# Two products for three, ScalarE's first parts ahead of POOL, and a weight ring of three and three slots

## What is computed

```python
h = rms_norm(x, pre_norm_gain); proj = h @ w_in            # q k v z_a b c u z_c, 512 columns each
mixed = concat([attn, conv_out]) @ w_out; x = x + rms_norm(mixed, post_norm_gain)
x = x + sigmoid(x @ w_ple_gate) * rms_norm(p @ w_ple_proj, ple_norm_gain)
n = rmsnorm(h, norm_mix); parts = n @ w_in2                # c_q c_kv k_pe gq gk gv ga gg gate_a gate_b
mix = sigmoid(gate_a) * (y_a @ w_o_mla) + sigmoid(gate_b) * (y_b @ w_o_gla); h = h + mix @ w_out2
q = rmsnorm(h, norm_ffn) @ w_q; s = q . sub_keys; top 16 of 128 for both halves, then top 16 pairs
out = sum over experts of gate * gelu(h . u) * v           # dense here: 16384 experts in 128 tiles
```

## Time and profile before

| | before |
|---|---|
| median of 3 runs | 2176.15 us |
| span of the profiled execution | 2175.93 us |
| TensorE busy | 2115.4 us, 97% |
| VectorE, ScalarE, POOL busy | 1304.1, 922.6, 1033.5 us |
| DMA | 359 MB, 165 GB/s in the mean |

### The profile page before, as it was taken

The page is one execution under the profiler, slowest core; times in us unless marked ns, Lnnn a source line. Parts: engine busy times, 40 slices in busy tenths (PEclk is TensorE's granted clock), DMA queues, the critical chain, the costliest instruction groups (busy, mean ns, idle before and its releaser), DMA issues.

```text
span 2175.9 us, 27394 instructions
## 1 busy us (share of the span) xinstructions
PE 2115.4 (97%) x10296; PEld 1661.6 (76%) x10296; DVE 1304.1 (60%) x2244; ACT 922.6 (42%) x1528; POOL 1033.5 (47%) x892
## 2 busy tenths in 40 slices
PE   8999999999999999999999998999999899999999
PEld 6877767557887776887878877777778788888887
DVE  6456257352235774215898957888881666666664
ACT  4223343572234234111334447777773434343432
POOL 6655546212324122877859887999996100000000
PEclk9999999999999999999999999999999999999999
DMA  5222312201111111233216664777788988888884
GB/s 201 100 78 78 116 61 90 90 30 49 59 40 59 59 55 43 97 122 110 78 59 199 205 206 141 272 289 246 272 291 294 333 300 286 289 284 300 288 287 149
DMA packets 98291, 359.32 MB, mean 165 GB/s; under 512 B 8480, under 2 KB 41504, under 8 KB 73328
## 3 DMA queue, kind: packets, MB, share of 16 engines
q1 hardware_dynamic: 98160, 357.56, 47.3%
HBM read 286.09 MB, written 71.30 MB: 164 GB/s over the span
## 4 chain that ended last, share of the span: by engine, by line
PE 67%; POOL 13%; DVE 11%; issue 6%; ACT 2%; DMA 1%; POOLq 0%; SPq 0%; ACTq 0%; DVEq 0%
PE ps L1438 11%; PE ps L1439 11%; PE ps L802 10%; PE ps L803 9%; PE ps L804 9%; POOL area L2643 6%; POOL wring_parts L2621 6%; PE ps L791 2%; PE ps L1249 2%; DVE area L2413 2%; PE ps L1386 1%; PE ps L1387 1%; DVE area L2410 1%; PE ps L884 1%; PE ps L1225 1%
## 5 line engine op out<-in xcount | busy, mean ns | idle before, releaser
L2577 POOL CAST wring_parts<-wring 128x512 fp32r<-128x512 f32 x236 | 170.5, 764 | 546.0 <-PE ps L804 429.3
L1386 PE MATMUL ps<-sqbuf_parts,wring_parts 128*128 128x512 f32 x1024 | 412.6, 403 | 5.5 <-POOL wring_parts L2621 5.5
L1387 PE MATMUL ps<-normed_x_parts,wring_parts 128*128 128x512 f32 x1024 | 404.4, 395 | 0.0
L2621 POOL TENSOR_TENSOR wring_parts<-wring_parts,wring 128x512 fp32r<-128x512 f32 x256 | 331.0, 1323 | 76.0 <-ACT wring_parts L1856 73.0
L2581 POOL TENSOR_TENSOR wring_parts<-wring,wring_parts 128x512 fp32r<-128x512 f32 x244 | 351.2, 1470 | 6.6 <-ACT wring_parts L1852 1.5
L1386 PEld LDWEIGHTS ps<-sqbuf_parts,wring_parts 128*128 128x128 f32 x1024 | 194.0, 189 | 50.6 <-POOL wring_parts L2621 4.9
L1387 PEld LDWEIGHTS ps<-normed_x_parts,wring_parts 128*128 128x128 f32 x1024 | 193.9, 189 | 41.8
L802 PE MATMUL ps<-resid_parts,wring_parts 128*128 128x512 f32 (+1 forms) x528 | 201.2, 381 | 6.1 <-DVE normed_x_parts L2010 3.3
L803 PE MATMUL ps<-normed_x_parts,wring_parts 128*128 128x512 f32 (+1 forms) x528 | 197.0, 373 | 0.0
L804 PE MATMUL ps<-resid_parts,wring_parts 128*128 128x512 f32 (+1 forms) x528 | 196.2, 372 | 0.0
L1474 ACT ACTIVATE area<-ps 128x1024 f32<-128x1024 f32 (+6 forms) x89 | 61.7, 696 | 275.2 <-PE ps L804 183.5
(11 more groups left out here) (269 smaller groups left out, 4431.4 us busy)
## 6 DMA issues: line engine op xcount, KB each, us to landing
wring<-in_weights_dram SPq DMA_DIRECT2D x65, 1024.0 KB, 4.8
wring<-in_uT_dram SPq DMA_DIRECT2D x128, 512.0 KB, 4.4
area<-in_vT_dram SPq DMA_DIRECT2D x44, 1024.0 KB, 7.2
hidden_table<-area SPq DMA_DIRECT2D x32, 1024.0 KB, 6.7
gate_table<-area SPq DMA_DIRECT2D x32, 1024.0 KB, 8.4
area<-gate_table SPq DMA_DIRECT2D x32, 1024.0 KB, 9.1
wring<-in_vT_dram SPq DMA_DIRECT2D x20, 1024.0 KB, 6.7
rt<-hidden_table SPq DMA_DIRECT2D x32, 512.0 KB, 4.6
```

The costliest lines, as they stand in the source:

```text
L1386: pe.matmul(out, first[:, d], h_first[:, k, :], start=(k == 0), stop=False)
L1387: mm = pe.matmul(out, rest[:, d], h_rest[:, k, :], start=False, stop=(k == KD - 1))
L2577: ins = nc.gpsimd.tensor_copy(up[:, d, :], W(name)[:, d, :])
L2621: ins = nc.gpsimd.tensor_tensor(rest[:, a:a + PIECE], first[:, a:a + PIECE], u_raw[t % len(USLOT)][:, a:a + PIECE], ALU.subtract)
```

## The change

- `three` becomes `two`. A part pair is now first part = 127/128 of the value for weights, 1/128 for activations, both rounded, and rest = first - value for weights, 127 x first - value for activations (the gains `pre`, `mix` and `ffn` are multiplied by 128 at the start, and readers of these products multiply by 128 where they did not). The product is first x first + rest x rest: two matmuls.
- POOL multiplies by GAIN where it copied.
- For 30 groups (`AHEAD_W`: wo2, wo3, pg0 to pg3, cq0, cq1, gg2, gg3, tb, ob, w2, pq) ScalarE makes the first part in two halves (`round_ahead`), at places written out in its list; it waits there for the weight and for the slot. POOL waits for `ahead_up` and only subtracts.
- The ring has three arriving slots and three for first parts. `USLOT` is computed from where pq5, pq6 and pq7 lie, and the first six table tiles are loaded two each when pq5, pq6 and pq7 are finished, where it was pq4 to pq7 with 1, 1, 2, 2.

The diff, cut to its core:

```diff
-USLOT = (1, 2, 3, 5, 0, 4)
-NW = 4
-NU = 2
+NW = 3
+NU = 3
+USLOT = [slot for n in (5, 6, 7) for slot in (WN[f"pq{n}"] % NW, NW + SPLIT.index(f"pq{n}") % NU)]
+AHEAD_W = ([f"wo{m}" for m in (2, 3)] + [f"pg{m}" for m in range(4)] + ["cq0", "cq1", "gg2", "gg3", "tb0", "ob0", "tb1", "ob1"]
+           + ["tb2", "ob2", "tb3", "ob3"] + [f"w2{m}" for m in range(4)] + [f"pq{m}" for m in range(HP)])
...
-            for n, tiles in enumerate(((0,), (1,), (2, 3), (4, 5))):
-                when_filled(sp, ("pq", HP - 4 + n))
+            for n, tiles in enumerate(((0, 1), (2, 3), (4, 5))):
+                when_filled(sp, ("pq", HP - 3 + n))
...
-            def three(out, a_parts, b_parts, first, last):
-                (a_up, a_low), (b_up, b_low) = a_parts, b_parts
-                pe.matmul(out, a_up, b_up, start=first, stop=False)
-                pe.matmul(out, a_up, b_low, start=False, stop=False)
-                return pe.matmul(out, a_low, b_up, start=False, stop=last)
+            def two(out, a_parts, b_parts, first, last):
+                (a_first, a_rest), (b_first, b_rest) = a_parts, b_parts
+                pe.matmul(out, a_first, b_first, start=first, stop=False)
+                return pe.matmul(out, a_rest, b_rest, start=False, stop=last)
...
+            def round_ahead(name):
+                i = SPLIT.index(name)
+                up, _ = W_parts(name)
+                act.wait_ge(w_in[WN[name] % NW], 16 * (WN[name] // NW + 1))
+                when_filled(act, last_job(SPLIT[i - NU]))
+                for half in (slice(0, KD // 2), slice(KD // 2, KD)):
+                    act.activation(up[:, half, :], W(name)[:, half, :], ACT.Copy, scale=GAIN).then_inc(ahead_up, 1)
...
             for m in range(4):
                 when_filled(act, ("wo", m))
-                square_two("post", m, pair(("wo", m)))
-                copy_out(("wo", m), mixedT[:, 2 * m:2 * m + 2, :], pair(("wo", m)))
+                round_ahead(("wo2", "wo3", "pg0", "pg1")[m])
+                square_two("post", m, pair(("wo", m)), scale=float(SCALE))
+                copy_out(("wo", m), mixedT[:, 2 * m:2 * m + 2, :], pair(("wo", m)), scale=float(SCALE))
...
             for m in range(4):
-                copy_out(("pg", m), sgT[:, 2 * m:2 * m + 2, :], pair(("pg", m)), ACT.Sigmoid)
+                round_ahead(("pg2", "pg3", "cq0", "cq1")[m])
+                copy_out(("pg", m), sgT[:, 2 * m:2 * m + 2, :], pair(("pg", m)), ACT.Sigmoid, float(SCALE))
...
+            round_ahead("gg2")
             silu(0)
             root("g2", T)
             root("g3", T)
             for h in range(HG):
                 if h + 1 < HG:
+                    round_ahead(("gg3", "tb0", "ob0")[h])
                     silu(h + 1)
                 round_pair(8 + h, O_PARTS, 2 * h, oT)
+            round_ahead("tb1")
             sigmoid(0)
             for m in range(4):
+                round_ahead(("ob1", "ob2", "ob3", "w21")[m])
                 if m + 1 < 4:
+                    round_ahead(("tb2", "tb3", "w20")[m])
                     sigmoid(m + 1)
                 round_pair(12 + m, MIX_PARTS, 2 * m, mixT)
             for m in range(4):
+                round_ahead(("w22", "w23", "pq0", "pq1")[m])
                 when_emptied(act, ("w2", m))
...
             for m in range(4):
                 round_pair(16 + m, Q_PARTS, 2 * m, hs)
+            round_ahead("pq2")
+            round_ahead("pq3")
             act.activation(h_first, hs, ACT.Copy, scale=1.0 / SCALE).then_inc(h_rounded, 1)
...
-                if HP - 4 <= h < HP - 2:
...
-                    act.activation(W_parts(name)[0], W(name), ACT.Copy).then_inc(query_up, 1)
+                if 2 <= h < HP - 2:
+                    round_ahead(f"pq{h + 2}")
...
-                dve.tensor_tensor(parts[1][:, k:k + 2, :], src[:, k:k + 2, :], parts[0][:, k:k + 2, :],
-                                  ALU.subtract).then_inc(pair_split, 1)
+                dve.scalar_tensor_tensor(parts[1][:, k:k + 2, :], parts[0][:, k:k + 2, :], float(SCALE - 1),
+                                         src[:, k:k + 2, :], ALU.mult, ALU.subtract).then_inc(pair_split, 1)
...
-                if i >= len(SPLIT) - 2:
-                    pool.wait_ge(query_up, i + 3 - len(SPLIT))
-                else:
+                ahead = name in AHEAD_W
+                if not ahead:
                     for d in parts:
-                        ins = nc.gpsimd.tensor_copy(up[:, d, :], W(name)[:, d, :])
+                        ins = nc.gpsimd.tensor_scalar(up[:, d, :], W(name)[:, d, :], GAIN, None, ALU.mult)
...
                 for d in parts:
-                    ins = nc.gpsimd.tensor_tensor(low[:, d, :], W(name)[:, d, :], up[:, d, :], ALU.subtract)
+                    if ahead and d.start in (0, k // 2):
+                        pool.wait_ge(ahead_up, 2 * AHEAD_W.index(name) + (1 if d.start == 0 else 2))
+                    ins = nc.gpsimd.tensor_tensor(low[:, d, :], up[:, d, :], W(name)[:, d, :], ALU.subtract)
```

## The result

The changed kernel takes **2053 us** (median of four runs, 2050.7 to 2060.8) against 2176.2 before, a ratio of 0.9436 (95% interval 0.9412 to 0.9459). The forecast was 2005 with a range of 1984 to 2034, so the direction was right and 48 of the 171 us did not come. The profiled execution has a span of 2053.4 us.

A forecast was written before the change was run, and what follows sets the result against it. TensorE was taken to bound the kernel (busy 2115 of 2176 us), with a ceiling of 235 us for the removed matmuls. Gains by stage summed to 171.3 us, giving 2005 us, with 8 in 10 in 1984 to 2034.

The forecast's parts named there:

- Stage 7: gg, tb, ob, w2: 58.2 us less a longer w20 wait and contention, gain 55.8; load-and-parts loop of 11 to 12 fits.
- I take 0.6 to 0.8: Price in us of POOL's multiply per piece, between copy (0.57) and two-input subtraction (1.25 to 1.3).
- The first rival: POOL's multiply is dear, 1.3 to 1.5 us a piece, slowing front groups: 2020 to 2032 us; chance 0.17.
- Stage 1: First four groups, to q1's end: gain 9.8 us less 1.7 for TensorE's low clock, so 8.1.
- Stage 3: Output projection to second norm (wo, ple, pg, cq): 34.5 us of matmuls removed, four things late, gain 14.3.
- (a): Output projection: the last heads' VectorE chain, covered by 54 matmuls, is now covered by 36; 3.3 us lost.
- (b): wo2's first part, made by ScalarE only once wo0 is filled, is ready 6.4 us after that.
- (c): ScalarE waits for pg1's load ahead of the norm "post"'s last square; 2.7 us lost.
- (d): Gate loop: VectorE's own work read as 9.0 us; gates every 9.3 where TensorE would need 7.3; gain 6.7.
- Stage 6: Third attention (gv3, ta): TensorE already waits for VectorE in the first head; gain 16.3 us.
- the second rival: Ring of load, ScalarE (in order) and POOL binds, 9 us a group and not 7.3: 2032 us; chance 0.13.
- Stage 8: Queries: 29.1 us of matmuls removed, but ScalarE's queue and VectorE's top-k chain set what follows; gain 0.3.

The follow-up runs named there:

- e1: Changed kernel with POOL copying a weight into its first part where it multiplied by 127/128; 2018.8 us (0.926).
- e3: Changed kernel with ScalarE also making the first parts of k1 to wo1, so POOL there only subtracts; 2032.4 us (0.933).
- after: The changed kernel itself as measured and profiled, against the kernel before; 2053 us (0.9436).
- e9: Changed kernel with POOL's subtraction for pg2, pg3, cq0, cq1 cut to 16 columns, TensorE reading the first part for the rest; 2045.4 us (0.9392).
- e2: Kernel before, three products kept, with POOL multiplying by 1.0 where it copied; 2195.9 us (1.0081).
- e10: Kernel before, three products kept, with only the ring changed to three arriving slots and three for first parts; 2172.9 us (0.9976).
- e5: Changed kernel with ScalarE also making the first parts of ta1 to ta3, gg0 and gg1; 2031.3 us (0.9326).
- e6: Changed kernel with the ring as before the change, four arriving slots and two for first parts; 2046.1 us (0.9397).
- e4: Changed kernel with ScalarE's first parts of pg3, cq0, cq1 moved behind the previous gate's sigmoid and gg3 ahead of the last two heads' roots; 2055.3 us (0.9432).

## Why the prediction was wrong, step by step

Two steps failed. The price of POOL's multiply was taken at half of what it is (19.1 us by wo0), and what POOL's instructions do to VectorE's chains beside them was nowhere in the sum (most of the 25 us missing in stages 3 and 6). Stage 7's 10.0 us are mainly one first part that stood in ScalarE's list behind other work.

- **Ceiling and starts.** Right. No third matmul, and undisturbed runs still start 0.23 apart. Two products run as the table products did; that rival is gone.
- **"I take 0.6 to 0.8".** Wrong, and the largest single error: 1.47 us without company, 1.57 in the mean. The first rival stood at 1.3 to 1.5 with 2020 to 2032; the price alone lies in that, its mean a little above, and the effect that it named did come, 19.1 us by wo0. The reasoning "one input, so it is nearer to the copy" was the choice between two ends by likeness of operands; the row nearest by kind of work, the subtraction, was the better guide. The 769 ns that the Trainium skill gives for 512 elements (GPSIMD Engine Reference, 3.1 Elementwise) would make 0.77 us a piece; the measurement, 1.47, decides.
- **"The wider VectorE instructions ... hide in engines with idle time".** Right for these (1.23 us for 128x1024 alone, 1.22 before), but the step asked only about their own length. What POOL's instructions do to VectorE's was nowhere in the sum beyond "contention 1.1".
- **Stage 1, 8.1.** Came 5.3. v0 waited 4.9 us for POOL; with the copy (e1) q1 ends at 54.5, near the 54.0 of the step.
- **Stage 2, 41.** Came 24.7, by POOL's price; e1 44.4.
- **Stage 3, 14.3.** Came 3.3. By the step's own terms 3.7 + 7.3 - 2.7 is 8.3 and not 8.6, a slip that matters little. (a) was right in kind: with POOL out of the way (e3) the last heads' chain shows as a wait of 3.49 us, forecast 3.3; in after POOL's wait of 4.4 stands in its place. (b) was right: wo2 started 7 us after wo0 was filled (218.3 to 225.26), forecast 6.4. (c) was right: ScalarE stood at pg1's load, and the last square kept TensorE 3.10 us, forecast 2.7. (d) the spacing of the gates was right, 9.3 forecast, 9.2 measured on average (290.0 to 317.5 in three steps), and its meaning wrong: it is 9.2 because of POOL. The 9.0 us that the step read as VectorE's own work were already stretched by POOL, whose copies and subtractions ran beside them; in e9 the same five instructions take 5.3. The step left out that the first gate comes 4.1 us later behind the norm (9.53 for 5.4). The low clock, forecast at one drop and 1 us, took some 7: the 40 matmuls behind the wait of 4.4 us 1.6, wo2's and wo3's 64 another 1.6, the projection's 24 (12.50 us for 10.46) and pg3's 32 (9.65 for 7.63) 2.0 each.
- **Stage 4, 5.5.** Came 5.5.
- **Latents, 0.** 3.4 came, from the clock and not from the change. TensorE waits as much in both (4.2 and 4.1 us), but in the profiled execution of the kernel before the granted clock fell to 0.72 and 0.79 behind two waits of 1.96 and 2.26 us, 0.96 over the stage; after it was 1.00, behind a wait of 2.84 us too. e2 and e10, with three products, have 90.8 us at 1.00.
- **Stage 5, 30.** Came 29.4: the term, the loop of copy, exp and scale, and the loss of 1.6 held. The sum has a slip: 32 x 0.227 + 64 x 0.124 + 128 x 0.12 is 30.6 and not 31.6, so the step's own terms give 29.0.
- **Stage 6, 16.3.** Came 2.3. The step priced TensorE against VectorE's chain as it stood, and took the ring as harmless because a group's loop had room. It never asked **when** in a head POOL would work after the load had moved. e5 and e6 show that it was this: with the parts out of the chain 24.7 and 18.7 came. From gv3 to gg0 TensorE waited 11.5 us in after and 2.7 in e5; the other 13.6 of the 22.4 us between them are the low clock, for which this step had no term.
- **Stage 7, 55.8.** Came 45.8. The steady pace was right, POOL's groups are 7.4 apart (827.67, 835.05, 842.43 us). So was w20's wait, 3.32, forecast 3.1. Missed: gg3's first part stood behind two roots and five table loads (1.28 us each) on ScalarE, and TensorE waited:

```profile
803.98 0.76 PE L810 MATMUL ps<-resid_parts,wring_parts 128*128 128x512 f32 x1 [5.94 <-POOL wring_parts L2614]
```

  The low clock behind this wait and w20's added 2.7 us each. In e4 the wait is 3.1 and the stage 3.8 shorter. This is the second rival in its kind ("ScalarE in order") but at one place, not as a pace.
- **Stage 8, 0.3.** Came 2.8. The queue was as forecast: pq2's and pq3's first parts 3.88 us ahead of h_first, the copy of ps0 119.5 us earlier than before, as early as w23 was (119.7); the step had it 1.6 us later than that. Behind it the top-k chain was earlier by 119.6 at its start and 121.7 at its end, and the end by 122.5:

```profile
928.32 3.88 ACT L1525 ACTIVATE wring_parts<-wring 128x1024 fp32r<-128x1024 f32 x4
932.11 3.60 ACT L1869 ACTIVATE sqbuf_parts<-normed_x 128x4096 fp32r<-128x4096 f32 x1
935.62 1.00 ACT L1481 ACTIVATE area<-ps 128x1024 f32<-128x1024 f32 x1
```

- **The range.** Its upper end, 2034, stood just above the end of either rival alone (2032). POOL's price and a part of the ring case came together, and the third cause, VectorE held by POOL, was in no rival.

What is open: the 2 to 5 us by which the last stretch differs between kernels that are the same there (1143.8 to 1148.6 in after, e4, e5, e9), which swallowed e4's gain; why a wait of 2 us was followed by the low clock in some executions and not in others; and whether POOL's multiply is dear for its rounded output or for every output, which was not tried.

## What to carry to other kernels

When a bound is lifted, ask of every instruction that another engine issues not only how long it is, but which chain it will lie beside; a deeper or narrower ring moves transfers, and with them the work that follows them, by 20 us and more without a wait showing anywhere. Price an unknown POOL operation at no less than its dearest relative (here 1.3 us, and even that was below the 1.47). A wait in the trace is worth its length only if no longer chain stands beside it (e4), and what is won ahead of a VectorE-bound end is sure only once it exceeds some 4 us.

## What the runs showed of the hardware

- POOL's multiply by a constant, 512 elements a partition, f32 to fp32r: 1.47 us alone, against 0.57 for the copy; 5.4 to 5.8 us for 2048.
- A VectorE instruction of 0.35 us took 4.51 us and ended 0.08 us after POOL's instruction of 5.37 us. One with two inputs in SBUF, 0.69 us alone, ended 4.18 us after the start of such an instruction (3.22 us), and the next took 0.68 beside its end. Half the piece took VectorE's rows beside POOL from 1.88 and 2.17 us to 1.64 and 1.63, and cost POOL 0.87 us where half of 1.45 was due.
- A weight load of one product shifted in time changed a stretch of 151 us by 16 us, with hardly any engine's work changed (POOL 50.5 and 46.8 us busy).
- Behind waits of 3.3 and 5.9 us some 13 matmuls of TensorE started 0.43 us apart and not 0.23, which cost 2.7 us each time.
